# Spacing the activation chunks 1056 instead of 1024 bytes apart in SBUF

## The reference, cut to what matters

```python
proj = h @ w_in[l]                      # 1024 -> 3584
up = causal_dwconv(h @ w_up[l], ...)    # 1024 -> 5632
f = (jax.nn.gelu(gt) * v) @ w_down[l]   # 2816 -> 1024
proj = x @ w_in                         # delta rule, 1024 -> 4112
q, k, v = jnp.split(x @ w_qkv, 3, axis=-1)
def swiglu(x, w13, w2):                 # twice, 1024 -> 5632, 2816 -> 1024
    g, u = jnp.split(x @ w13, 2, axis=-1)
    return (jax.nn.silu(g) * u) @ w2
```

## The kernel before

| operand | before | after |
|---|---|---|
| `hi`, `lo`, `raw`, every piece | 0 | 0 |
| `hh` and `hl`, chunks 0 to 7 | 32 in all | 192, 224, 0, 32, 64, 96, 128, 160 |
| `fh`, chunks 0 to 3 | 64 in all | 192, 224, 0, 32 |
| `fl`, chunks 0 to 3 | 64 in all | 64, 96, 128, 160 |
| `idle`, `crow`, `xa`, `h`, `B`, `ev`, `Z`, `cst` | 64 | 192 (640 bytes further) |

## Time and profile before

### The profile page before, as it was taken

The page is one execution under the profiler, slowest core; times in us unless marked ns, Lnnn a source line. Parts: engine busy times, 40 slices in busy tenths (PEclk is TensorE's granted clock), DMA queues, the critical chain, the costliest instruction groups (busy, mean ns, idle before and its releaser), DMA issues.

```text
span 1167.3 us, 20553 instructions
## 1 busy us (share of the span) xinstructions
PE 1109.0 (95%) x8544; PEld 1068.4 (92%) x8544; DVE 807.5 (69%) x1360; ACT 614.9 (53%) x1028; POOL 3.3 (0%) x13
## 2 busy tenths in 40 slices
PE   7998989999999998879989999999999999999997
PEld 7998878899999987679989999999999799999996
DVE  7988489877878787586666755555589656555555
ACT  5567444555555648742454554545455545545453
POOL 0000000000000000000000000000000000000000
PEclk9999999999999998989989999999999999999998
DMA  9985247257666523234224266565536332665620
GB/s 377 418 314 179 74 145 279 95 175 246 229 223 210 180 76 113 61 102 146 73 73 143 70 205 198 183 197 184 160 120 201 130 128 91 217 198 181 197 75 37
DMA packets 58557, 195.60 MB, mean 168 GB/s; under 512 B 10848, under 2 KB 11232, under 8 KB 58208
## 3 DMA queue, kind: packets, MB, share of 16 engines
q1 hardware_dynamic: 58464, 194.28, 49.1%
HBM read 192.94 MB, written 1.31 MB: 166 GB/s over the span
## 4 chain that ended last, share of the span: by engine, by line
PE 73%; DVE 17%; ACT 7%; issue 2%; SPq 1%; DMA 0%; POOL 0%; ACTq 0%; DVEq 0%; POOLq 0%
PE ps L512 61%; DVE lo L1475 4%; PE ps L725 3%; ACT hi L1008 2%; DVE raw L1462 2%; PE ps L610 2%; PE ps L519 2%; DVE B L1484 1%; PE ps L531 1%; DVE ev L1713 1%; DVE st L1492 1%; PE ps L507 1%; DVE ev L1710 1%; DVE B L1788 1%; DVE B L1497 1%
## 5 line engine op out<-in xcount | busy, mean ns | idle before, releaser
L512 PE MATMUL ps<-hh,hi 128*128 128x256 f32 x1792 | 511.2, 285 | 15.2 <-DVE hl L1509 3.5
L512 PE MATMUL ps<-hh,lo 128*128 128x256 f32 x1792 | 504.3, 281 | 0.0
L512 PE MATMUL ps<-hl,hi 128*128 128x256 f32 x1792 | 503.9, 281 | 0.0
L1475 DVE TENSOR_TENSOR lo<-raw,hi 128x1024 fp32r<-128x1024 f32 x311 | 378.2, 1222 | 171.9 <-ACT hi L1008 171.1
L512 PEld LDWEIGHTS ps<-hh,hi 128*128 128x128 f32 x1792 | 340.7, 190 | 19.9 <-issue 9.6
L1008 ACT ACTIVATE hi<-raw 128x1024 fp32r<-128x1024 f32 x311 | 324.2, 1051 | 51.9 <-PE ps L512 51.6
L512 PEld LDWEIGHTS ps<-hl,hi 128*128 128x128 f32 x1792 | 340.6, 190 | 1.1
L512 PEld LDWEIGHTS ps<-hh,lo 128*128 128x128 f32 x1792 | 340.7, 190 | 0.0
L512 PE MATMUL ps<-fh,hi 128*128 128x256 f32 x392 | 109.9, 280 | 3.9 <-ACT B L1112 2.9
L512 PE MATMUL ps<-fh,lo 128*128 128x256 f32 x392 | 108.8, 278 | 0.0
L512 PE MATMUL ps<-fl,hi 128*128 128x256 f32 x392 | 108.8, 277 | 0.0
(11 more groups left out here) (256 smaller groups left out, 1221.8 us busy)
## 6 DMA issues: line engine op xcount, KB each, us to landing
raw<-in_w SPq DMA_DIRECT2D x359, 512.0 KB, 4.2
B<-in_t SPq DMA_DIRECT2D x2, 512.0 KB, 4.8
xa<-in_x SPq DMA_DIRECT2D x1, 1024.0 KB, 10.4
B<-in_r SPq DMA_DIRECT2D x1, 1024.0 KB, 6.0
out<-h SPq DMA_DIRECT2D x4, 256.0 KB, 2.0
cst<-in_c SPq DMA_DIRECT2D x1, 864.0 KB, 8.3
B<-between SPq DMA_DIRECT2D x32, 4.0 KB, 1.6
vec<-in_v SPq DMA_DIRECT2D x1, 328.5 KB, 6.7
```

The source lines that it names most:

```text
L512: m = g.matmul(o, l, r, start=first and n == 0, stop=last and n == 2, skip_group_check=True)
L1475: g.tensor_tensor(lo[:, j % SPLIT, :], raw[:, PLACE[j] % RAW, :], hi[:, j % SPLIT, :].bitcast(F), ALU.subtract).then_inc(*up("lo", j))
```

## The change

The rows of `hh`, `hl`, `fh` and `fl` become 264 words long, and only the first 256 of each are used. The two gaps go. The two instructions of the delta rule that wrote two chunks as one flat run of 512 now write them as 2 x 256. No instruction is added, removed or moved: instruction for instruction the engines' programs are the same but for these two shapes and the addresses.

```diff
         ones = sb("ones", [P, 3, P])
-        gap0 = sb("gap0", [P, 24])
-        hh = sb("hh", [P, NC, S], FR)
-        hl = sb("hl", [P, NC, S], FR)
-        gap1 = sb("gap1", [P, 8])
-        fh = sb("fh", [P, 4, S], FR)
-        fl = sb("fl", [P, 4, S], FR)
+        hh = sb("hh", [P, NC, S + 8], FR)[:, :, 0:S]
+        hl = sb("hl", [P, NC, S + 8], FR)[:, :, 0:S]
+        fh = sb("fh", [P, 4, S + 8], FR)[:, :, 0:S]
+        fl = sb("fl", [P, 4, S + 8], FR)[:, :, 0:S]
         idle = sb("idle", [P, S], FR)
...
-                g.activation(x[:, 2 * u:2 * u + 2, :].rearrange("p a b -> p (a b)"), bank[b][:, :], ACT.Copy,
+                g.activation(x[:, 2 * u:2 * u + 2, :], pair(b), ACT.Copy,
                              scale=V("a_norm_g")).then_inc(*up("gh", u))
...
-                g.scalar_tensor_tensor(out=xl[:, v, :].rearrange("p a b -> p (a b)"), in0=bank[b][:, :],
-                                       scalar=V("a_norm_g"), in1=xh[:, v, :].rearrange("p a b -> p (a b)").bitcast(F),
+                g.scalar_tensor_tensor(out=xl[:, v, :], in0=pair(b),
+                                       scalar=V("a_norm_g"), in1=xh[:, v, :].bitcast(F),
                                        op0=ALU.mult, op1=ALU.subtract).then_inc(*up("gl", u))
```

## The result

The median goes from 1171.46 to 1181.43 us (1179.88 to 1181.47, 3 runs), 10 us more. The ratio of the two means is 1.0077, with a 95% interval of 1.0054 to 1.010, which is 9 us, between 6.3 and 11.7. The forecast was slower, by 5.9 us, to 1177.4.

What follows compares the result with a forecast made beforehand. TensorE, busy 95%, was taken to bound the kernel through the split products' pitch. Steps 5.3 plus fh/fl 1.9, times 0.82, gave +5.9 us on 1171.5: 1177.4 us, 8-in-10 range 1165 to 1184.

Steps and rivals of the forecast that it cites:

- The settled price: Split products with hh/hl: mean pitch over the eight distances 116.8 ns, the price of now, so nothing added.
- the five unknown distances: Operand distances 96 to 224, in no profile row; taken at 116.5 ns, with bounds 113.3 and 119.7.
- The steps: Tiles: changing distance every three matmuls costs 1.2 ns on each of 4416 matmuls, +5.3 us.
- `fh` and `fl`: Their 1176 split matmuls go from 115.4 to 117.0 ns by their own distances, +1.9 us.
- Exposure, 0.82: Share of the split products' pitch change reaching the end: 712 us on the chain of 871 us of matmuls.
- Zeros: No cost taken for 512-wide matmuls, float32 matmuls, reshaped instructions, or VectorE and ScalarE writing to other bytes.
- Clean far distances: Rival: split-product reads half a cycle apart meet less, settled mean 114.8 ns; 1161.5 us, or 1166.5; chance 0.25.
- As dear as 0: Rival: unknown distances cost split products what 0 does, mean 118.8 ns; 1183 to 1187 us; chance 0.12.
- Chance rhythms: Rival: distance doesn't matter to split products, pitch levels are chance; time within 2 us of 1171.5; chance 0.2.

Runs made afterwards that it cites:

- dist: Kernel before plus some 2400 dummy matmuls at stepped operand distances; moving operand further: 119.9 ns at 0, 116.7 at 32; stepping 118.3 ns; no kernel time given.
- hh_only: Kernel before with only hh and hl spaced 1056 bytes apart at the change's remainders; 1.0067 of before (1.0047 to 1.0086), +7.8 us.
- fh_only: Kernel before with only fh and fl spaced 1056 bytes apart at the change's remainders; 1.0018 of before (1.0005 to 1.0032), +2.1 us.
- hh96: Kernel before, 1024-byte spacing kept, with hh and hl moved from remainder 32 to 96; 1.0154 of before (1.0137 to 1.0171).
- all112: Kernel before, 1024-byte spacing kept, with hh, hl, fh and fl all at remainder 112; 0.9899 of before (0.9881 to 0.9917), 1160.2 us.
- tail_only: Kernel before with 128 unused bytes behind fl, moving the later tensors from remainder 64 to 192; 0.9998 of before (0.9984 to 1.0012).
- tail_back: Changed kernel with 128 unused bytes behind fl, returning the later tensors to remainder 64; 1.0074 of before (1.0056 to 1.0092).
- hh112: Kernel before, 1024-byte spacing kept, with hh and hl moved from remainder 32 to 112; 0.9928 of before (0.9916 to 0.9940).
- weights96: Kernel before with the 96-byte gap moved ahead of hi, so weights go from remainder 0 to 96, activations staying; 0.9967 (0.9952 to 0.9981), -3.9 us.
- all192: Kernel before, 1024-byte spacing kept, without gaps ahead, hh, hl, fh and fl all at remainder 192; 0.9934 of before (0.9917 to 0.9951).

## Why the prediction was right

**Direction and mechanism.** Slower, because the split products' pitch follows the distance between the two operands by 256, and the change gives up a better than average distance of `hh` and `hl`, 32, for the whole cycle. The single distances show it (`dist`: 116.7 ns at 32 against a mean of 117.8), and so do `hh_only` and the constant remainders on either side of the change. The size was too small, 5.9 us against 9 (6.3 to 11.7), and that it came so near owes something to luck, as the next points say.

**The settled price.** This term was too small. With 116.5 for the five unknown distances the mean came to 116.8, no more than before. The mean of the eight is 117.8 in the dummy stream: 96 at 120.0, 128, 160 and 224 at 118.5, 117.3 and 118.3, only 192 cheap, and 64 at 117.8 instead of the 115.4 taken. The 1.0 ns was left out of the tiles, and out of `rows_in` and the tiles made together too, where nothing was taken and 0.7 ns measured.

**The steps.** This term was too large: 1.2 ns taken, 0.5 measured by `dist`. The two errors nearly cancel, which is luck: tiles at 118.1 expected (116.9 and 1.2), 118.5 measured. The reading of the earlier trace rows as a price of each step is not borne out. The 120 ns behind `fh` may be a stream that finds another rhythm; no run singles it out.

**`fh` and `fl`.** +1.6 ns taken, +2.3 measured; 1.9 us expected at full exposure and 2.7 found. The sign was right and the reason only in part: the term was worked out from the distances of `fh` and `fl` themselves, but `hh_only` leaves these at 64 and its `fh` units rise to 117.8 ns all the same. Alone, their spacing costs 2.1 us (`fh_only`, 0.6 to 3.7); on top of the spacing of `hh` it adds next to nothing. How the neighbouring stream decides the rhythm of `fh` stays open.

**Exposure, 0.82.** Fits the change, 8.3 us by pitches and 9 measured, but the interval leaves any share from 0.6 up, and it is no constant: `hh96` shows 0.96 and `all112` 0.64. Where nothing is exposed is where the earlier trace rows said: instructions 1477 to 2343 took 105.0 us before and after.

**Zeros.** `tail_only` and `tail_back` confirm the tensors behind, and with them the float32 matmuls and the engines' work on those tensors; the layer norm's matmuls have a pitch of 215.8 ns before and 215.9 after. The 512-wide matmuls went from 233 to 232 ns, and the reshaped ScalarE instruction from 689 and 688 ns to 687 and 682.

**The rivals.** Clean far distances: false. The five unknown ones average 117.6 ns (moving), not under 114.8; of them only 192 is cheap, and 96 is as dear as 0. As dear as 0: false for all but 96. Chance rhythms: half true, since 64, 112 and 192 each have two, and the `fh` units change theirs with the neighbour; but a set of prices belongs to each distance. The Trainium skill's independent read ports ("TensorE: Matmul & The Clock Gate", "Step-by-step: what each phase is for") don't explain why `hh96` and `hh112`, which differ in nothing but start bytes, are 2.3% apart; here the measurements decide. That the weight load and the moving read get in each other's way is what `weights96` suggests, but no run looked at it directly, and why 112 and 96 differ so stays open.

## What to carry to other kernels

Where split or other full-rate matmuls fill TensorE, the start-to-start pitch is the first number to take, in a window of one kind, and it can be some per cent too long with every engine's figures in order. Try the start of the activation tensor against that of the weights in steps of 16 bytes; a stream of dummy matmuls in front of the kernel prices all sixteen distances in one run. Then choose one constant distance and keep it for all chunks, since an even mixture pays the mean and most distances are dear; and look at the real kernel's trace for a second rhythm before believing the price. Look there at the streams that were not touched as well: one operand's new place changed the rhythm of the other's products. And when two parts of a change are measured apart, compare the same pieces of work in their traces before adding the parts up.

## What the runs showed of the hardware

The settled pitch of a 128 x 256 fp32r matmul at full clock lies between 113.3 and 120.0 ns by the start bytes of its operands, with two levels at some distances; at half clock a pitch is mostly 213 to 214 ns, in the traces of before and of the change alike. A rhythm once taken can last for stages (`all192`, 113.3 or 117.8).

Two profiled executions of the same speed can differ by several us in where TensorE's clock stands at half. The profile of `tail_only` has a span of 1173.0 us and 119 split matmuls with a pitch between 205 and 222 ns, that of before 1167.3 us and 72, while their medians are the same. So 12.4 us between the spans of before and changed is not the change's price alone: the changed kernel's profile has 127 such matmuls. Windows of the kernel before; the third number from the end is TensorE's granted clock:

```profile
412.00:520.00 108.00, 90.33 (x606) 82.81 (x605) 77.81 (x181) 71.46 (x126) 2.02 (x1) 0.94 0.26 81
520.00:660.00 140.00, 134.17 (x1114) 132.43 (x1113) 94.33 (x179) 60.26 (x105) 0.00 (x0) 0.98 0.28 94
```

The same windows of the changed kernel, with less of the clock granted in both:

```profile
412.00:520.00 108.00, 91.82 (x600) 84.15 (x598) 77.09 (x178) 69.88 (x124) 2.02 (x1) 0.92 0.28 87
520.00:660.00 140.00, 134.01 (x1086) 132.26 (x1085) 92.45 (x177) 57.33 (x101) 0.00 (x0) 0.95 0.29 96
```
